# Order of the first loads and column blocks in a fused two-block transformer kernel

## The reference

```python
silu_c  = silu(c);  silu_cc = silu(c_ctx)
mod   = silu_c  @ w_mod + b_mod          # 6 * 1024 columns
mod_c = silu_cc @ w_mod + b_mod
sh1, sc1, gt1, sh2, sc2, gt2 = split(mod, 6)

h  = rms_norm(x,   g_pre1) * (1 + sc1)  + sh1
hc = rms_norm(ctx, g_pre1) * (1 + sc1c) + sh1c
qn, kn, vn, qh, zf, zb, ih, gh = split(h @ w_in, 8)      # 512 columns each
_,  kn_c, vn_c, _, zf_c, zb_c, ih_c, _ = split(hc @ w_in, 8)
# attention in a window with axial rotation of qn and kn, gated linear attention in
# chunks, output projection, 16 experts of 32 tokens each, then the second block
```

## Time and profile before

| what | us |
|---|---|
| median of 3 runs (2890.18 to 2895.75) | 2893.08 |
| the profiled execution | 2895.4 |
| its span, first to last instruction | 2893.6 |
| TensorE busy | 2220.4 |
| VectorE busy | 647.5 |
| ScalarE busy | 332.0 |
| start of column block 0 | 48.63 |
| end of block 7, about | 259.9 |

### The profile page before, as it was taken

One profiled execution on the slowest core, in us unless ns is written; L12 is line 12 of the kernel. 1 busy time (PEld: TensorE's weight loads), 2 busy tenths in 40 slices (PEclk: granted clock), 3 DMA queues, 4 the chain that ended last, 5 costly groups with the idle time before them and its releaser, 6 DMA issues.

```text
span 2893.6 us, 35403 instructions
## 1 busy us (share of the span) xinstructions
PE 2220.4 (77%) x15652; PEld 1296.3 (45%) x15652; DVE 647.5 (22%) x1143; ACT 332.0 (11%) x604; POOL 118.0 (4%) x103
## 2 busy tenths in 40 slices
PE   5999786655566666678888755788886999867998
PEld 2444463222222322234444322635774884645873
DVE  1111552101011111122222100644442000631000
ACT  2001321000010000011011000312112000221000
POOL 0001100000000000001111000000220000100000
PEclk8999887999999999999999999878998999888999
DMA  8445612899999999999999999435301463302450
GB/s 338 179 151 193 229 55 78 353 422 425 424 424 422 421 418 421 424 408 424 425 424 424 424 425 412 139 130 176 117 1 58 149 215 110 117 31 87 146 210 22
DMA packets 158889, 755.93 MB, mean 261 GB/s; under 512 B 12233, under 2 KB 75721, under 8 KB 102033
## 3 DMA queue, kind: packets, MB, share of 16 engines
q1 hardware_dynamic: 158736, 753.67, 65.7%
HBM read 752.58 MB, written 1.05 MB: 260 GB/s over the span
## 4 chain that ended last, share of the span: by engine, by line
PE 51%; DMA 38%; DVE 6%; ACT 3%; issue 2%; POOL 0%; DVEq 0%; SPq 0%; ACTq 0%; POOLq 0%
DMA ring<-w_up_dram 13%; DMA ring<-w_gate_dram 12%; PE psum L530 11%; PE psum L473 10%; DMA ring<-w_down_dram 9%; PE psum L557 5%; DMA ring<-hyb_w_dram 3%; PE psum L1025 3%; PE psum L414 2%; PE psum L1414 2%; PE psum L393 2%; PE psum L1133 2%; PE psum L1089 1%; PE psum L1480 1%; PE psum L864 1%
## 5 line engine op out<-in xcount | busy, mean ns | idle before, releaser
L1025 PE MATMUL psum<-ring,arena 128*32 128x320 f32 x4096 | 359.1, 467 | 283.0 <-DMA ring<-w_up_dram 142.9
L530 PE MATMUL psum<-arena,ring 128*128 128x256 f32 x1408 | 307.7, 382 | 5.6 <-issue 5.6
L1025 PEld LDWEIGHTS psum<-ring,arena 128*32 128x32 f32 x4096 | 112.2, 111 | 441.2 <-DMA ring<-w_up_dram 174.8
L1089 PE MATMUL psum<-ring,arena 128*32 128x512 f32 x1344 | 211.7, 603 | 108.3 <-DMA ring<-w_down_dram 108.3
L530 PEld LDWEIGHTS psum<-arena,ring 128*128 128x128 f32 x1408 | 269.7, 192 | 43.4 <-issue 6.2
L473 PE MATMUL psum<-ring,arena 128*128 128x512 f32 x608 | 275.5, 615 | 13.1 <-ACT arena L2500 5.0
L473 PEld LDWEIGHTS psum<-ring,arena 128*128 128x128 f32 x608 | 119.4, 198 | 166.0 <-issue 166.0
L393 PE MATMUL psum<-consts,arena 128*128 128x128 f32 x550 | 101.2, 332 | 120.1 <-DVE arena L1564 71.5
L1089 PEld LDWEIGHTS psum<-ring,arena 128*32 128x32 f32 x1344 | 47.5, 109 | 248.1 <-DMA ring<-w_down_dram 173.2
L393 PEld LDWEIGHTS psum<-consts,arena 128*128 128x128 f32 x550 | 81.0, 180 | 173.1 <-DVE arena L1564 70.6
L557 PE MATMUL psum<-ring,arena 128*128 128x512 f32 x352 | 151.4, 592 | 0.0
(11 more groups left out here) (357 smaller groups left out, 2103.5 us busy)
## 6 DMA issues: line engine op xcount, KB each, us to landing
ring<-w_gate_dram SPq DMA_DIRECT2D x128, 1376.0 KB, 18.2
ring<-w_up_dram SPq DMA_DIRECT2D x128, 1376.0 KB, 18.2
ring<-w_down_dram SPq DMA_DIRECT2D x112, 1536.0 KB, 20.0
ring<-w_mod_dram SPq DMA_DIRECT2D x72, 1024.0 KB, 5.0
ring<-w_ffn_in_dram SPq DMA_DIRECT2D x88, 512.0 KB, 5.1
ring<-w_ffn_out_dram SPq DMA_DIRECT2D x14, 1536.0 KB, 6.7
ring<-w_in_dram SPq DMA_DIRECT2D x16, 1024.0 KB, 5.3
ring<-hyb_w_dram SPq DMA_DIRECT2D x10, 1024.0 KB, 16.8
```

The lines of the kernel that those rows point to most:

```text
L530: ins = nc.tensor.matmul(b[:, i * 256:(i + 1) * 256], ws[k // 4][:, k % 4, u, i * P:(i + 1) * P], R(XT + k * 256, 256), start=(k == 0), st ...
L1025: ins = nc.tensor.matmul(banks[u][c][32 * j:32 * j + 32, 0:GMAIN], R(XST + k * HALF + e * CAP, CAP), w3[:, 64 * c:64 * c + 64, QGROUP * j: ...
L1089: ins = nc.tensor.matmul(ybanks[half][32 * c:32 * c + 32, :], stationary, w, start=((half, c) not in begun), stop=(unit >= 36), skip_group ...
```

## The change

The identity is loaded by itself, ahead of x, and counted by a semaphore of its own; the rest of the constants is loaded later. ScalarE and VectorE no longer wait for `rows` or for the constants ahead of x. TensorE transposes x behind modulation part 5. The column blocks run in the order 0, 3, 1, 2, 4, 5, 6, 7, and the 16 remaining modulation parts stand in groups of 3, 5, 4 and 4 behind the second to the fifth of these. The ctx transfer moves behind the weights of block 0, `rows` behind the fourth block and its parts. The modulation's columns and gates stand together behind block 5.

```diff
+        IN1 = (0, 3, 1, 2, 4, 5, 6, 7)
+        WITH_CTX = (1, 2, 4, 5, 6)
+        MOD1_AT = {1: range(0, 3), 2: range(3, 8), 3: range(8, 12), 4: range(12, 16)}
...
 # TensorE
             for k in range(KT):
                 modulation_part("mod1", 0, k, 6, "c1")
-            pe.wait_ge(consts_loaded, 16 * tally.due(consts_loaded))
-            normalised_T("x1", XN)
+                if k == 5:
+                    pe.wait_ge(ident_loaded, 16 * tally.due(ident_loaded))
+                    normalised_T("x1", XN)
             modulation_cols("mod1", 0)
             transposed("x1")
-            for c in range(8):
-                project("in1", c, range(4) if c in (1, 2, 4, 5, 6) else range(2), HALF)
-                if c < 4:
-                    for k in range(4 * (c % 2), 4 * (c % 2) + 4):
-                        modulation_part("mod1", 1 + c // 2, k, 7 - c // 2, "c1")
-                if c == 0:
+            for i, c in enumerate(IN1):
+                project("in1", c, range(4) if c in WITH_CTX else range(2), HALF)
+                for n in MOD1_AT.get(i, ()):
+                    modulation_part("mod1", 1 + n // KT, n % KT, 7 - n // KT, "c1")
+                if i == 0:
                     normalised_T("ctx1", XN)
+                elif i == 1:
                     transposed("ctx1")
-                elif c == 4:
+                    pe.wait_ge(consts_loaded, 16 * tally.due(consts_loaded))
+                elif i == 5:
                     modulation_cols("mod1", 1)
                     modulation_cols("mod1", 2)
-                elif c == 5:
                     modulation_gates("mod1")
...
 # VectorE
-            v.wait_ge(consts_loaded, 16 * tally.due(consts_loaded))
             v.wait_ge(cols_loaded, 16 * tally.due(cols_loaded))
-            v.wait_ge(rows_loaded, 16 * tally.due(rows_loaded))
             v.wait_ge(x_loaded, 16 * tally.due(x_loaded))
             normalise(X, XN)
...
+                if i == 0:
+                    v.wait_ge(consts_loaded, 16 * tally.due(consts_loaded))
...
-                if c in (1, 3):
-                    modulation_rows("mod1", MB, 1 + c // 2)
-                elif c == 4:
+                if i in (2, 4):
+                    modulation_rows("mod1", MB, i // 2)
+                elif i == 5:
...
             lb, oml = R(WP, HALF), R(WT, HALF)
+            v.wait_ge(rows_loaded, 16 * tally.due(rows_loaded))
...
 # ScalarE
-            a.wait_ge(rows_loaded, 16 * tally.due(rows_loaded))
             a.wait_ge(x_loaded, 16 * tally.due(x_loaded))
...
 # SyncE
             mod_in("mod1", T["w_mod"], 0, 0, 3)
-            load(consts[:, :], T["consts"], consts_loaded)
+            load(consts[:, 0:P], T["consts"][:, 0:P], ident_loaded)
             rows_in(x[:, :], T["x"], x_loaded)
...
-            load(rows[:, :], T["rows"].partition_broadcast(P), rows_loaded)
-            rows_in(R(CX, 2048), T["ctx"], ctx_loaded)
-            for c in range(8):
+            for i, c in enumerate(IN1):
                 proj_in("in1", T["w_in"], c * 512, 512, c)
-                if c < 4:
-                    mod_in("mod1", T["w_mod"], 1 + c // 2, 4 * (c % 2), 4 * (c % 2) + 4)
-                if c == 0:
+                if i == 0:
+                    rows_in(R(CX, 2048), T["ctx"], ctx_loaded)
+                    load(consts[:, P:], T["consts"][:, P:], consts_loaded)
+                for n in MOD1_AT.get(i, ()):
+                    mod_in("mod1", T["w_mod"], 1 + n // KT, n % KT, n % KT + 1)
+                if i == 0:
                     post_rows(T["g_post1"], T["g_post2"])
+                elif i == 3:
+                    load(rows[:, :], T["rows"].partition_broadcast(P), rows_loaded)
```

More of the change, by code:

```diff
@@ L145, in program @@
         pool_done = semaphore("pool_done")
+        ident_loaded = semaphore("ident_loaded")
         consts_loaded = semaphore("consts_loaded")
@@ L2558, in _ @@
             modulated_T("ctx1", 16, 0, 1, XT, 512, 256)
-            for i, c in enumerate((1, 2, 4, 5, 6)):
+            for i, c in enumerate(WITH_CTX):
                 for t in range(2, 4):
```

## The result

The changed kernel takes 2873.03 us in the median (2872.78 to 2874.32, 4 runs) against 2894.16 (2890.18 to 2895.75, 4 runs): ratio 0.993, 95% interval 0.9914 to 0.9946. That is 21 us less; 2883.1 was forecast, with a range of 2877.5 to 2889.0, so the time lies outside it on the good side.

What follows compares the result with a forecast made beforehand. Transfers and what follows them bound the first 48.6 us, then TensorE, later TensorE and DMA in turns. Terms 4.1 - 0.7 + 7.5 - 0.9 gave 10.0 us less, a median of 2883.1 us, range 2877.5 to 2889.

Steps and rivals of the forecast that it cites:

- Constants split: Start of the kernel: 1730.5 KB of constants leave the queue ahead of x and modulation parts 3 to 7, gaining 4.1 us.
- Transposes between the parts: Start: the 16 transposes of x behind modulation part 5 delay part 7, costing 0.7 us, at most 1.2.
- the tail: From part 7's end to VectorE's read of the last transpose: 1.8 us instead of 9.34, gaining 7.5.
- The rival reading, that transposes leave the clock down: Transposes of x run at half clock: the slow price of 1.2 us, forecast 0.5 us later; no chance given.
- Rows and context later: Projection: ctx, rows and the remaining constants, loaded later, still arrive before they are needed; cost 0.
- two blocks without context first: Before block 3: the 4.2 us idle and the clock's return of 2.4 and 2.9 us stay, each 2 us either way.
- The ring: Before block 2: its weights, issued when block 1 ends, stall TensorE 0.9 us behind five modulation parts; ends 0.2 and 6.
- Columns and gates: Behind block 5: standing together they cost 0, perhaps gain 0.6 us; the 2.9 us wait before the gates stays.
- The sum at block 6: Projection: gains and losses of the terms, 4.1 - 0.7 + 7.5 - 0.9, make 10.0 us less.
- a lead that TensorE wins at the start is handed on: Expert stage: weight transfers are issued when TensorE frees a ring slot, so the 10 us lead reaches the end.
- One of the prediction's own signs of being wrong: Whole trace: the forecast is wrong if the lead at the first expert is not the lead at the end.
- rival E: Start and projection: TensorE busy from part 4 to 7 makes both clock returns, 2.4 and 2.9 us, vanish; 2878, chance 0.05.

Runs made afterwards that it cites:

- second pair: Both kernels run and traced once more with no edit: the kernel before 2891.19 us, the changed kernel 2872.63 us, ratio 0.9936.

## Why the prediction was wrong

**Constants split: right.** x landed at 3.25 + 11.8 = 15.05 (14.8 forecast), part 7's matmuls began at 28.49 instead of 32.43, 3.9 earlier (4.1).

**Transposes between the parts: wrong sign.** I took 0.7 us of loss. They cost nothing, and they kept TensorE at full clock, so that part 7 took 1.06 instead of 1.93: 0.9 won. Part 7 ended at 29.55, not 31.0. With the tail right (29.55 to 31.52 is 2.0 against 1.8 forecast) and 31.52 to 36.45 unchanged at 4.93, block 0 started 12.2 us earlier, not 10.9. The rival reading, that transposes leave the clock down, is refuted here: granted 1.00 in 24 to 26 with TensorE transposing for nearly all of it, and down from 28 on in the kernel without them there. The Trainium skill, "TensorE: Matmul & The Clock Gate", Part 4: PE-mode transpose, states that the full clock does not engage for transposes; these traces show otherwise.

**Rows and context later, two blocks without context first: right.** No wait for ctx or constants; block 3 waited 3.89 us for VectorE (4.2 forecast). The clock's return cost 15.53 - 13.83 = 1.7 us instead of 2.9, within the 2 us that I had left open.

**The ring: right.** 1.03 us of stall (0.9), and 4.50 of five parts in front of it. Columns and gates 3.74 (199.82 to 203.56) against 0.94 + 2.86 before: nothing.

**The sum at block 6** is then 13.1 where mine gave 10.0. It would have given a median of 2880, inside the range. (The gain's lower end of 8.5 does not come out of the terms' ends as given: 3.8 - 1.2 + 7.5 is 10.1, and less a stall of 0.9 or 6 that leaves 9.2 or 4.1. The miss is on the other side.)

**The step that failed** is the one that I put as "a lead that TensorE wins at the start is handed on". It is handed on through the experts (D, within 1 us), but not through the sections where TensorE works in short pieces between waits. There the granted clock falls at some waits and not at others. Which ones differs between two runs of one kernel as well, so that the shifted start changed it is my reading and not shown. I counted the clock only for blocks 0 and 3, with 2 us for each, and the rest of the kernel at zero and without a bound. In the first pair of traces it was worth 9 us, and half of the time that TensorE was busy at the lower level in B, C and E fell by 10.0; in the second pair it was 4, and 4.4. Between the medians it was 8 and 5. One of the prediction's own signs of being wrong came true: the lead was 18.2 at the first expert and 22.3 at the end. In rival E I had the mechanism with the right sign and the wrong place: it gave 5 us in the projection and 0.05 of the chance.

Shown: most of what B, C and E differ by goes with the time at the lower granted clock. Shown too: the drop at the start of attention costs 4.8 us in B where it comes at its usual length (16.8 against 12.0), and it was absent in all five traces with one or two matmuls in the wait ahead of it, one of the kernel before and four of the changed one. Not shown: that its price reaches the end; with three matmuls before block 3, taking it away won 6.3 us in B and nothing in the rest. Shown again: the levels of two lists of work repeat (2873.0 and 2872.6; 2878.8 and 2879.3), while that of before came out between 2891.2 and 2895.2, and small edits of the order move the level by 5 to 6 us with A unchanged. Open: which waits a drop follows, and why the changed list is at the low end in every run, though its drops differ from one run to the next. Theory L, that the length of work since the last return of the clock decides, foretold none of three kernels.

## What to carry to other kernels

Take away waits that lump transfers together: a 64 KB piece that is needed first does not belong in a 1.8 MB transfer, and work on data that has long landed belongs in the gaps of an engine that waits for a stream; here it also kept the clock up. Give a time forecast a term for the clock over the whole kernel, not only near the edit: two traces of one unchanged kernel give its size (here 4 us, over 12 us of spread). And when a result is well above the structural sum, look for the lead at fixed instructions along the trace before crediting the edit; here 5 to 8 of the 19 to 21 us are nowhere near it, and as much is lost when a reorder that saves nothing by itself is undone. When extra instructions stand between two records, count them out: the same count from the end then points at another record.

## What the runs showed of the hardware

The same kernel ran in 2883.91 to 2895.87 over 11 runs with nothing changed, and another list with 13 us less at its start in 2871.28 to 2873.48 over 5. Adding work can save time where it is added: with two matmuls more, the 60 records behind them took 9.7 us instead of 14.4, and the whole 3.8 less by the ratio. And four matmuls (3.60 us) behind block 7 cost 9.6 in the traces and 9.4 in the medians. In 19 traces, sections of TensorE's work in short pieces differ by up to 12.7 us; less half of the time that it was busy at the lower of the clock's two levels, by 4.8.
